# End of the even mixer in a hybrid decoder step: the prompt states of the retention heads go to PSUM bank 0, and norms, roots and roundings are written in another order

## The chip, the cores and the metric

The kernel runs on one core of one Trainium2 chip. The metric is the device time of one execution in microseconds; for the kernel before it is the median of three executions.

## What is computed

One inference step of a two-layer decoder for 512 prompt positions and 8 sample positions that share all weights. Layer 0 has, between two feed-forward blocks, the even mixer: one input projection feeds four retention heads and four HGRN2 heads of 128 x 128, each head's output is normalised and multiplied by a gate, and one output projection takes all eight. Cut to what the change touches:

```python
def even_mixer(h, pos, S_ret0, S_hg0, w_in, w_out, ret_g, hg_g, lb):
    rq, rk, rv, rg, gq, gf, gi, gg = jnp.split(h @ w_in, splits, axis=-1)
    o_r, S_ret = retention_scan(q, k, v, S_ret0, log_gamma)
    o_r = head_norm(o_r, ret_g, False).reshape(B, T, -1) * jax.nn.silu(rg)
    o_g, S_hg = hgrn2_scan(qq, kk, logf, vv, S_hg0)
    o_g = head_norm(o_g, hg_g, False).reshape(B, T, -1) * jax.nn.sigmoid(gg)
    y = jnp.concatenate([o_r, o_g], axis=-1) @ w_out
    return y, S_ret, S_hg
# head_norm: x * lax.rsqrt(jnp.mean(x * x, axis=-1) + EPS) * g
```

## The kernel before

The kernel is one program per engine, written out by hand in order; the engines meet only through semaphores (`wait_ge` ahead of an instruction, `then_inc` on the one that releases). Nothing schedules: the order of the work on an engine is the order of the code. Activations lie transposed, features on partitions and the 520 positions along the free axis. Every large projection multiplies a 128-column unit of the weight, split by ScalarE and VectorE into a rounded part and a rest (`hi`, `lo`), with the likewise split activations, three products for each pair: `three` for most projections, `out_e` for the mixer's output projection.

The change lies between the last unit of the mixer's input projection and the output projection. There a loop over the four retention heads h runs on three engines.

- **TensorE** (from L2143): four score products of head h (L2149, 512, 384, 256 and 128 columns, into banks 1 to 3), the transposes of keys and values of head h+1 (L2100, L2102), the product of weighted scores and values (L2162, bank 6 or 7), the prompt state of head h (L2167, four accumulating 128-column products), and the sum of squares of head h-1 over partitions by a product with ones (L2171). Behind the loop stand 32 one-column products with sample states (L2083), the last sum of squares (L2176), and then the output projection: unit 0 over the four HGRN2 heads, a small sum for the samples (L2089), unit 1 over the HGRN2 heads, then both units over the retention heads, then units 2 to 7 (all L2187).
- **VectorE** (from L1561): `decayed(h)` multiplies the scores by the decay table (L1532, four pieces), `ret_keys(h+1)` scales the transposed keys (L1490), `ret_state(h)` copies the state out of PSUM (L1540). Between them stand `hgrn_norm` for the last HGRN2 head (L1413, L1414), `gated(t)`, which multiplies head t by its gate (L1554; t is 0 to 3 for retention, 4 to 7 for HGRN2), `head_low(t)`, the rest after rounding (L1559), and `ret_norm(h)`: a reciprocal (L1545) and a multiplication (L1546). `sample_out` and `sample_low` do the same for the 8 sample positions.
- **ScalarE** (from L912): it copies the transposed values out (L917), squares the head's output and copies it out of PSUM (L926, L927), takes the root of the sum of squares (`ret_root`, L906), and rounds finished heads (`head_high`, L901).

Buffers tie them together. The state of head h lies in bank 3, in the columns behind the last two score products, and before the next head's scores TensorE waits for its copy:

```python
out = ps[:, min(c + 1, 3), c // 3 * 2 * P:c // 3 * 2 * P + n]
if h and c == 0:
    pe.wait_ge(S("r_p"), NC * h)
    pe.wait_ge(S("st_out"), NH + h)
```

The product of weighted scores and values of heads 2 and 3 writes the PSUM bank that holds head h-2's sum of squares, so it waits for that head's root (`r_sd`). The squares of heads 2 and 3 reuse the buffer that holds the reciprocal root of head h-2, so ScalarE's square waits until that head is normalised and gated (`hn_y`). The weighted scores of head h overwrite those of head h-1, so `decayed(h)` waits for `r_pv`. The two halves of the retention part of the output projection wait for all retention heads and the samples (`hn_lo`, `es_lo`).

## Time and profile before

| | |
|---|---|
| median of 3 executions | 2556.22 us (2552.15 to 2558.25) |
| the profiled execution's own time | 2556.56 us |
| its span | 2554.7 us |
| TensorE busy, share of the span | 2431.4 us, 95% |
| VectorE busy | 1372.7 us, 54% |
| ScalarE busy | 772.8 us, 30% |
| mean granted clock of TensorE | 0.98 |

The span is the time between the first and the last instruction of the profile; 1.9 us of the execution lie around it. Busy TensorE is not TensorE at its peak, since matmuls are pipelined and their ends are modelled. The granted clock is the share of full speed that the engine was given; 0.50 is 1.2 GHz and 1.00 is 2.4 GHz. In the timelines an idle time in square brackets stands ahead of the instruction that ended it, with what released it.

### The profile page before, as it was taken

What the parts mean: (1) busy time and instruction counts of PE and PEld (TensorE: products, weight loads), DVE (VectorE), ACT (ScalarE), POOL (GpSimd) and SP (SyncE); (2) the same over time, 40 slices, a digit from 0 to 9 for tenths busy, and PEclk for the clock granted to TensorE, in tenths of its full rate; (3) what the DMA queues carried; (4) which work ended last, traced back from release to release, by engine and by line L of the source; (5) the groups of instructions that cost most, each with busy time, mean ns of one, the idle gap of its engine ahead of it and who ended that gap; (6) DMA issues with size and microseconds to landing.
All of it is one profiled execution on the core that took longest, in us unless ns stands there. A gap on an engine that the chain in (4) does not pass through costs nothing.

```text
span 2554.7 us, 44447 instructions
## 1 busy us (share of the span) xinstructions
PE 2431.4 (95%) x18881; PEld 2306.1 (90%) x18881; DVE 1372.7 (54%) x1816; ACT 772.8 (30%) x1049; POOL 353.8 (14%) x494
## 2 busy tenths in 40 slices
PE   7999999999889999999999999999988879999999
PEld 6999999999779999999999999887555579999998
DVE  4334334587565444334333437632888855666654
ACT  3222223443323222223222223234333222222222
POOL 1000000232001123000000000001221102444432
PEclk9999999999989999999999999999999899999999
DMA  3333334232114555332333332222444525989974
GB/s 108 91 90 90 104 90 132 76 94 76 45 43 145 160 160 115 96 90 83 90 90 95 101 87 83 83 74 50 129 149 149 157 82 188 297 293 297 300 242 166
DMA packets 444570, 325.19 MB, mean 127 GB/s; under 512 B 14713, under 2 KB 391845, under 8 KB 444301
## 3 DMA queue, kind: packets, MB, share of 16 engines
q1 hardware_dynamic: 427512, 274.90, 36.6%
q0 software_dynamic: 13232, 42.10, 4.6%
q10 hardware_dynamic: 3728, 6.87, 0.8%
q8 instruction: 63, 1.03, 0.2%
q14 instruction: 35, 0.29, 0.0%
HBM read 278.95 MB, written 44.99 MB: 127 GB/s over the span
## 4 chain that ended last, share of the span: by engine, by line
PE 85%; DVE 9%; ACT 2%; issue 2%; DMA 1%; POOL 0%; SPq 0%; DVEq 0%; ACTq 0%; POOLq 0%
PE ps L1921 71%; PE ps L2399 3%; PE ps L2187 2%; PE ps L2373 1%; PE ps L2024 1%; DVE m_qcs L1686 1%; PE ps L2327 1%; DMA m_c_ring<-in_state_mlstm_C 1%; PE ps L2344 1%; DVE m_w_lo L1171 1%; PE ps L2300 0%; PE ps L1985 0%; ACT m_w_hi L700 0%; PE ps L2312 0%; PE ps L2311 0%
## 5 line engine op out<-in xcount | busy, mean ns | idle before, releaser
L1921 PE MATMUL ps<-m_n_hi,m_w_hi 128*128 128x260 f32 x3808 | 772.9, 284 | 13.1 <-DVE m_w_lo L1171 11.5
L1921 PE MATMUL ps<-m_n_hi,m_w_lo 128*128 128x260 f32 x3808 | 768.9, 284 | 0.0
L1921 PE MATMUL ps<-m_n_lo,m_w_hi 128*128 128x260 f32 x3808 | 768.0, 283 | 0.0
L1921 PEld LDWEIGHTS ps<-m_n_hi,m_w_hi 128*128 128x128 f32 x3808 | 589.6, 189 | 16.6 <-DVE m_w_lo L1171 8.9
L1171 DVE TENSOR_TENSOR m_w_lo<-m_w_raw,m_w_hi 128x1024 fp32r<-128x1024 f32 (+1 forms) x312 | 408.3, 1309 | 364.5 <-ACT m_w_hi L700 359.8
L1921 PEld LDWEIGHTS ps<-m_n_hi,m_w_lo 128*128 128x128 f32 x3808 | 588.9, 189 | 0.0
L1921 PEld LDWEIGHTS ps<-m_n_lo,m_w_hi 128*128 128x128 f32 x3808 | 588.0, 189 | 0.0
L700 ACT ACTIVATE m_w_hi<-m_w_raw 128x1024 fp32r<-128x1024 f32 (+1 forms) x312 | 347.6, 1114 | 233.8 <-PE ps L1921 222.7
L1921 PE MATMUL ps<-m_h_hi,m_w_hi 128*128 128x260 f32 x1408 | 283.8, 283 | 0.0
L1921 PE MATMUL ps<-m_h_hi,m_w_lo 128*128 128x260 f32 x1408 | 283.1, 282 | 0.0
L1921 PE MATMUL ps<-m_h_lo,m_w_hi 128*128 128x260 f32 x1408 | 282.5, 282 | 0.0
L1921 PEld LDWEIGHTS ps<-m_h_lo,m_w_hi 128*128 128x128 f32 x1408 | 217.3, 188 | 0.0
L1921 PEld LDWEIGHTS ps<-m_h_hi,m_w_hi 128*128 128x128 f32 x1408 | 216.7, 188 | 0.0
L1921 PEld LDWEIGHTS ps<-m_h_hi,m_w_lo 128*128 128x128 f32 x1408 | 216.6, 188 | 0.0
L733 ACT ACTIVATE m_h_hi<-m_tmp 128x520 f32 (+1 forms) x88 | 56.2, 639 | 370.3 <-DVE m_tmp L1221 370.3
L729 ACT ACTIVATE m_tmp<-m_tmp 128x520 f32<-128x520 f32 x88 | 56.3, 640 | 345.1 <-DVE m_tmp L1206 345.1
L1206 DVE TENSOR_TENSOR m_tmp<-ps,m_rstd 128x520 f32<-128x520 f32 x88 | 61.5, 699 | 161.6 <-PE ps L1921 161.5
L1221 DVE TENSOR_TENSOR m_tmp<-m_tmp,ps 128x520 f32<-128x520 f32 x88 | 61.2, 696 | 148.1 <-PE ps L1921 146.7
L663 POOL TENSOR_SCALAR m_u_ring<-m_u_ring,m_ab 128x512 f32<-128x512 f32 x128 | 100.6, 786 | 230.4 <-DMA m_u_ring<-in_state_mlstm_C 227.7
L709 ACT ACTIVATE m_n_hi<-m_x,m_vec 128x520 fp32r<-128x520 f32 x48 | 35.1, 730 | 276.1 <-DVE m_x L1277 192.2
L1223 DVE TENSOR_TENSOR m_h_lo<-m_tmp,m_h_hi 128x520 fp32r<-128x520 f32 (+1 forms) x88 | 61.9, 704 | 74.8 <-ACT m_h_hi L733 74.8
L1275 DVE TENSOR_TENSOR m_tmp<-ps,m_rstd 128x520 f32<-128x520 f32 x32 | 22.4, 700 | 146.4 <-PE ps L1921 146.4
(432 smaller groups left out, 2573.6 us busy)
## 6 DMA issues: line engine op xcount, KB each, us to landing
m_w_raw<-in_ffn_w_gate SPq DMA_DIRECT2D x88, 512.0 KB, 3.9
m_w_raw<-in_ffn_w_up SPq DMA_DIRECT2D x88, 512.0 KB, 3.8
m_w_raw<-in_ffn_w_down SPq DMA_DIRECT2D x64, 704.0 KB, 4.6
m_c_ring<-in_state_mlstm_C SPq DMA_DIRECT2D x128, 256.0 KB, 3.4
m_u_ring<-in_state_mlstm_C SPq DMA_DIRECT2D x128, 256.0 KB, 6.0
out_C_s<-m_u_ring POOLq DMA_DIRECT2D x128, 256.0 KB, 5.4
m_w_raw<-in_ev_w_in SPq DMA_DIRECT2D x32, 512.0 KB, 4.0
m_w_raw<-in_ml_w_in SPq DMA_DIRECT2D x32, 512.0 KB, 4.0
```

The costliest lines, as they stand in the source:

```text
L663: nc.gpsimd.tensor_scalar(u_ring[:, n % UR, :], u_ring[:, n % UR, :], ab[:, h, 0, b:b + 1], 0.0, ALU.mult, ALU.add)\
L700: nc.scalar.activation(w_hi[:, j % 2, 0:kt * P], w_raw[:, j % 2, 0:kt * P], ACT.Copy).then_inc(S("w_hi"), 1)
L709: nc.scalar.activation(n_hi[:, k, :], x[:, k, :], ACT.Copy, scale=vec1[:, GAIN[s] + k:GAIN[s] + k + 1]).then_inc(S("xn_hi"), 1)
L729: nc.scalar.activation(tmp[c][:, :], tmp[c][:, :], ACT.Silu).then_inc(S("silu"), 1)
L733: nc.scalar.activation(h_hi[:, bass.ds(2 * i + c, 1), :].rearrange("p a t -> p (a t)"), tmp[2 + c][:, :], ACT.Copy).then_inc(S("h_hi"), 1)
L1171: v.tensor_tensor(w_lo[:, j % 2, 0:kt * P], w_raw[:, j % 2, 0:kt * P], w_hi[:, j % 2, 0:kt * P].bitcast(F32), ALU.subtract).then_inc(S("w_ ...
L1206: v.tensor_tensor(two(tmp[c][:, :]), pair(2 * c), by_rstd, ALU.mult).then_inc(S("g_r"), 1)
L1221: v.tensor_tensor(two(tmp[2 + c][:, :]), two(tmp[c][:, :]), pair(2 * c + 1), ALU.mult).then_inc(S("h_f"), 1)
L1223: v.tensor_tensor(h_lo[:, bass.ds(2 * i + c, 1), :].rearrange("p a t -> p (a t)"), tmp[2 + c][:, :], h_hi[:, bass.ds(2 * i + c, 1), :].rea ...
L1921: last = mm(out[:, t, :], w[:, j % 2, c], r[:, k0 + k, t * HT:(t + 1) * HT], start=start and k == 0 and n == 0, stop=stop and k == kt - 1 ...
L2187: last = mm(pair(OUT_E[d])[:, t, :], w[:, d % 2, c], r[:, t * HT:(t + 1) * HT], start=start and k == NH and n == 0, stop=k == NH - 1 and n ...
L2399: last = mm(pair(d % 4)[:, t, :], w[:, i % OS, c], r[:, 4 * q + k, t * HT:(t + 1) * HT], start=q == 0 and k == 0 and n == 0, stop=q == 3 a ...
```

## The change

The prompt states of the retention heads go to bank 0, columns 0 to 127. TensorE's wait for the state copy of head h-1 moves from the scores of head h to the state product of head h; head 0's state product waits for the root of the sample values that lie in bank 0, and the wait for the last copy stands ahead of the one-column products. On VectorE each state copy is moved behind the next head's `decayed` and `ret_keys`, and norms, gates and roundings move behind the loop or one head later. On ScalarE the root of head h-1 is taken ahead of the square of head h for heads 2 and 3, and behind the square for head 1, and the roundings are ordered anew. No instruction is added or taken away, except for waits.

```diff
--- before.py
+++ after.py
@@ -916,6 +916,15 @@
                         act.wait_ge(S("r_st"), h)
                     nc.scalar.activation(r_vtok[(h + 1) % 2], ps[:, 5, :].rearrange("p (c v) -> p c v", c=NC), ACT.Copy)\
                         .then_inc(S("r_vt"), 1)
+                if h == 2:
+                    head_high(NH + 1)
+                if h == 3:
+                    head_high(NH + 2)
+                    head_high(NH + 3)
+                if h >= 2:
+                    ret_root(h - 1)
+                if h == 3:
+                    head_high(0)
                 act.wait_ge(S("r_pv"), h + 1)
                 if h == 0:
                     act.wait_ge(S("g_pv"), NH)
@@ -925,18 +934,16 @@
                     act.wait_ge(S("hn_y"), NH + h - 1)
                 nc.scalar.activation(r_sqb[h % 2][:, :], ps[:, 6 + h % 2, :], ACT.Square)
                 nc.scalar.activation(rv[:, h, 0:TP], ps[:, 6 + h % 2, :], ACT.Copy).then_inc(S("r_o"), 1)
-                if h == 0:
+                if h == 1:
                     sample_high(1)
-                if h:
-                    ret_root(h - 1)
-                head_high(NH + h)
+                    head_high(NH)
+                    ret_root(0)
+            head_high(1)
             ret_root(NH - 1)
-            for t in range(NH):
-                head_high(t)
-                if t == 1:
-                    sample_root(0)
-                if t == 2:
-                    sample_high(0)
+            sample_root(0)
+            head_high(2)
+            sample_high(0)
+            head_high(3)
             for d in range(KD):
                 if 2 <= d + 1 < KD:
                     hi(first_unit["out_e"] + d + 1, (d + 1) % 2, KD)
@@ -1537,7 +1544,7 @@
                 dve.wait_ge(S("r_st"), h + 1)
                 if h == 0:
                     dve.wait_ge(S("st_p_sent"), 16 * NH)
-                v.tensor_copy(st_out[:, h, :], ps[:, 3, 3 * P:TP]).then_inc(S("st_out"), 1)
+                v.tensor_copy(st_out[:, h, :], ps[:, 0, 0:P]).then_inc(S("st_out"), 1)
 
             def ret_norm(h):
 
@@ -1563,28 +1570,30 @@
                 decayed(h)
                 if h + 1 < NH:
                     ret_keys(h + 1)
+                if h:
+                    ret_state(h - 1)
                 if h == 0:
                     lo(first_unit["out_e"] + 1, 1, KD)
                     hgrn_norm(NH - 1)
                     dve.wait_ge(S("g_nm"), NH)
+                if h == 1:
                     gated(NH)
                     sample_out(1)
-                ret_state(h)
-                if h == 1:
+                if h == 2:
                     gated(NH + 1)
                     gated(NH + 2)
                     head_low(NH)
                     sample_low(1)
-                if h == 2:
+                if h == 3:
                     gated(NH + 3)
-                    head_low(NH + 1)
                     ret_norm(0)
                     gated(0)
-                if h == 3:
-                    head_low(NH + 2)
-                    ret_norm(1)
-                    gated(1)
-                    head_low(NH + 3)
+                    head_low(NH + 1)
+            ret_state(NH - 1)
+            ret_norm(1)
+            gated(1)
+            head_low(NH + 2)
+            head_low(NH + 3)
             head_low(0)
             ret_norm(2)
             gated(2)
@@ -2143,7 +2152,6 @@
                     out = ps[:, min(c + 1, 3), c // 3 * 2 * P:c // 3 * 2 * P + n]
                     if h and c == 0:
                         pe.wait_ge(S("r_p"), NC * h)
-                        pe.wait_ge(S("st_out"), NH + h)
                     if h == 0 and c < 2:
                         pe.wait_ge(*evicted(30 + c))
                     mm(out, rk[:, h, c * P:(c + 1) * P], rq[:, h, c * P:TP], start=True, stop=True).then_inc(S("r_s"), 1)
@@ -2163,13 +2171,17 @@
                     at += TP - c * P
                 last.then_inc(S("r_pv"), 1)
                 pe.wait_ge(S("r_kd"), h + 1)
+                if h:
+                    pe.wait_ge(S("st_out"), NH + h)
+                else:
+                    pe.wait_ge(S("es_sd"), 1)
                 for c in range(NC):
-                    last = mm(ps[:, 3, 3 * P:TP], r_etok[h % 2][:, c, :], r_vtok[h % 2][:, c, :], start=c == 0, stop=c == NC - 1)
+                    last = mm(ps[:, 0, 0:P], r_etok[h % 2][:, c, :], r_vtok[h % 2][:, c, :], start=c == 0, stop=c == NC - 1)
                 last.then_inc(S("r_st"), 1)
                 if h:
                     pe.wait_ge(S("r_o"), h)
                     mm(ps[:, 6 + (h - 1) % 2, :], ones[:, :], r_sqb[(h - 1) % 2][:, :], start=True, stop=True).then_inc(S("r_ss"), 1)
-            pe.wait_ge(S("es_sd"), 1)
+            pe.wait_ge(S("st_out"), 2 * NH)
             for m in range(12, 16):
                 state_q(m)
             pe.wait_ge(S("r_o"), NH)
```

The first place is VectorE from the norm of the last HGRN2 head to the scores of retention head 1 (L1413 and L1414 the norm, L1554 its gate, L1467 the samples' reciprocal, L1532 the weighting of the scores). Before:

```order
L1413 RECIPROCAL m_sqb<-m_sqb 128x512 [waits s_g_sd]
L1414 SCALAR_TENSOR_TENSOR m_gi<-m_gi,m_vec_51,m_sqb 128x512 [waits s_dve_own]
L1554 TENSOR_TENSOR m_gi<-m_gi,m_gq 128x512 [waits s_g_nm]
L1467 RECIPROCAL m_qks<-m_qks 128x32 [waits s_es_sd]
L1475 TENSOR_TENSOR m_os<-m_os,m_ggx 128x8
L1540 COPY m_st_out<-ps 128x128 [waits s_st_p_sent,s_r_st]
L1532 TENSOR_TENSOR m_e_p<-ps,m_tab 128x512 [waits s_r_pv,s_r_s]
```

Of the change (L1420 and L1421 the norm, L1539 the weighting, L1497 the keys, L1547 the state copy, L1561 the gate, L1474 the samples):

```order
L1420 RECIPROCAL m_sqb<-m_sqb 128x512 [waits s_g_sd]
L1421 SCALAR_TENSOR_TENSOR m_gi<-m_gi,m_vec_51,m_sqb 128x512 [waits s_dve_own]
L1539 TENSOR_TENSOR m_e_p<-ps,m_tab 128x512 [waits s_r_pv,s_r_s,s_g_nm]
L1539 TENSOR_TENSOR m_e_p<-ps,m_tab 128x384 [waits s_r_s]
L1497 TENSOR_TENSOR m_e_tok<-ps,m_tab 128x512 [waits s_r_st,s_r_tr]
L1547 COPY m_st_out<-ps 128x128 [waits s_st_p_sent,s_r_st]
L1561 TENSOR_TENSOR m_gi<-m_gi,m_gq 128x512
L1474 RECIPROCAL m_qks<-m_qks 128x32 [waits s_es_sd]
```

The weighting of head 1 now stands straight behind the norm, and the state copy, the gate and the samples' operations stand behind it.

The second place is VectorE around the weighting of head 3 (L1532 before). Before, the norm and gate of head 0 (L1545, L1546, L1554) stand ahead of it:

```order
L1540 COPY m_st_out<-ps 128x128 [waits s_r_st]
L1554 TENSOR_TENSOR m_gi<-m_gi,m_ggx 128x512
L1559 TENSOR_TENSOR m_gi_lo<-m_gi,m_gk_hi 128x512 [waits s_hn_hi]
L1545 RECIPROCAL m_e_x<-m_e_x 128x512 [waits s_r_sd]
L1546 SCALAR_TENSOR_TENSOR m_rv<-m_rv,m_vec_51,m_e_x 128x512 [waits s_dve_own]
L1554 TENSOR_TENSOR m_rv<-m_rv,m_gf 128x512 [waits s_r_g,s_dve_own]
L1532 TENSOR_TENSOR m_e_p<-ps,m_tab 128x512 [waits s_r_pv,s_r_s]
L1532 TENSOR_TENSOR m_e_p<-ps,m_tab 128x128 [waits s_r_s]
L1540 COPY m_st_out<-ps 128x128 [waits s_r_st]
L1559 TENSOR_TENSOR m_gi_lo<-m_gi,m_gk_hi 128x512 [waits s_hn_hi]
L1545 RECIPROCAL m_sqb<-m_sqb 128x512 [waits s_r_sd]
```

Of the change, with its line numbers (L1539 weighting, L1547 state copy, L1552 and L1553 norm, L1561 gate, L1566 rounding rest):

```order
L1539 TENSOR_TENSOR m_e_p<-ps,m_tab 128x512 [waits s_r_pv,s_r_s]
L1539 TENSOR_TENSOR m_e_p<-ps,m_tab 128x128 [waits s_r_s]
L1547 COPY m_st_out<-ps 128x128 [waits s_r_st]
L1561 TENSOR_TENSOR m_gi<-m_gi,m_ggx 128x512
L1552 RECIPROCAL m_e_x<-m_e_x 128x512 [waits s_r_sd]
L1553 SCALAR_TENSOR_TENSOR m_rv<-m_rv,m_vec_51,m_e_x 128x512 [waits s_dve_own]
L1561 TENSOR_TENSOR m_rv<-m_rv,m_gf 128x512 [waits s_r_g,s_dve_own]
L1566 TENSOR_TENSOR m_gi_lo<-m_gi,m_gk_hi 128x512 [waits s_hn_hi]
L1547 COPY m_st_out<-ps 128x128 [waits s_r_st]
L1552 RECIPROCAL m_sqb<-m_sqb 128x512 [waits s_r_sd]
```

The norm of head 0 now stands behind the weighting of head 3, and the last state copy stands behind that norm instead of ahead of a rounding rest.

The third place is ScalarE after the square of head 1 (L926 square, L927 copy, L906 root, L901 rounding, L917 values). Before:

```order
L926 ACTIVATE m_sqb<-ps 128x512 [waits s_g_nm,s_r_pv]
L927 ACTIVATE m_rv<-ps 128x512
L906 ACTIVATE m_e_x<-ps,m_lbv 128x512 [waits s_r_ss]
L901 ACTIVATE m_gk_hi<-m_gi 128x512 [waits s_hn_y]
L917 ACTIVATE m_lev_88<-ps 128x512 [waits s_r_st,s_r_tr]
L926 ACTIVATE m_e_x<-ps 128x512 [waits s_hn_y,s_r_pv]
L927 ACTIVATE m_rv<-ps 128x512
L906 ACTIVATE m_sqb<-ps,m_lbv 128x512 [waits s_r_ss]
L901 ACTIVATE m_gk_hi<-m_gi 128x512 [waits s_hn_y]
L926 ACTIVATE m_sqb<-ps 128x512 [waits s_hn_y,s_r_pv]
```

Of the change (L935 square, L936 copy):

```order
L935 ACTIVATE m_sqb<-ps 128x512 [waits s_g_nm,s_r_pv]
L936 ACTIVATE m_rv<-ps 128x512
L896 ACTIVATE m_gk_hi<-m_os 128x4x8 [waits s_es_y]
L901 ACTIVATE m_gk_hi<-m_gi 128x512 [waits s_hn_y]
L906 ACTIVATE m_e_x<-ps,m_lbv 128x512 [waits s_r_ss]
L917 ACTIVATE m_lev_88<-ps 128x512 [waits s_r_st,s_r_tr]
L901 ACTIVATE m_gk_hi<-m_gi 128x512 [waits s_hn_y]
L906 ACTIVATE m_sqb<-ps,m_lbv 128x512 [waits s_r_ss]
L935 ACTIVATE m_e_x<-ps 128x512 [waits s_hn_y,s_r_pv]
L936 ACTIVATE m_rv<-ps 128x512
```

The root of head 1 (into `m_sqb`, L906) stood behind the square of head 2, and now stands ahead of it.

## Rows read from the trace of the kernel before

**Rows 1.** TensorE's timeline: start, us, operation xcount, idle ahead of it

```profile
666.20 2.52 PE L2149 MATMUL ps<-m_rq,m_rk 128*128 128x512 f32 x8
...
671.58 1.06 PE L2167 MATMUL ps<-m_v_tok,m_e_tok 128*128 128x128 f32 x8
677.58 4.61 PE L2149 MATMUL ps<-m_rq,m_rk 128*128 128x512 f32 x8 [4.94 <-DVE m_st_out L1540]
...
693.70 1.02 PE L2171 MATMUL ps<-m_sqb,m_ones 128*128 128x512 f32 x2
...
702.02 4.61 PE L2162 MATMUL ps<-m_e_p,m_lev 128*128 128x512 f32 x8 [5.14 <-ACT m_sqb L906]
...
708.74 4.75 PE L2083 MATMUL ps<-m_qs,m_e_ring 128*128 128x1 f32 x32
714.98 2.08 PE L2176 MATMUL ps<-m_sqb,m_ones 128*128 128x512 f32 x2 [1.49 <-ACT m_rv L927]
...
725.01 0.63 PE L2089 MATMUL ps<-m_qs,m_ones 128*128 128x32 f32 x2 [4.67 <-DVE m_qs L1462]
```

**Rows 2.** Windows: stretch, its length, busy of TensorE, PEld, VectorE, ScalarE, POOL, clock, DMA

```profile
677.00:684.00 7.00, 6.42 (x17) 4.53 (x18) 2.40 (x8) 0.84 (x3) 0.54 (x1) 0.52 0.03 9
...
725.00:731.00 6.00, 5.99 (x26) 5.69 (x26) 5.86 (x7) 0.80 (x2) 0.00 (x0) 0.50 0.00 0
760.00:1000.00 240.00, 240.00 (x1996) 239.78 (x1996) 116.36 (x175) 69.80 (x88) 57.41 (x108) 1.00 0.53 147
```

**Rows 3.** Who VectorE waited for, 666 to 734 us: total, times, longest

```profile
DVE m_st_out L1540 <- PE ps L2167: 11.0, 3, 6.3
...
DVE m_e_p L1532 <- PE ps L2149: 3.9, 5, 2.2
DVE m_rv_lo L1559 <- ACT m_rq_hi L901: 2.4, 2, 1.6
DVE m_gi_lo L1559 <- ACT m_gk_hi L901: 2.3, 1, 2.3
DVE m_e_tok L1490 <- PE ps L2102: 1.1, 1, 1.1
DVE m_lev L1490 <- PE ps L2102: 0.3, 1, 0.3
```

**Rows 4.** ScalarE's timeline: the squares of heads 2 and 3

```profile
700.26 0.60 ACT L926 ACTIVATE m_e_x<-ps 128x512 f32<-128x512 f32 x1 [8.82 <-DVE m_rv L1554]
...
713.84 0.60 ACT L926 ACTIVATE m_sqb<-ps 128x512 f32<-128x512 f32 x1 [11.40 <-DVE m_rv L1554]
```

**Rows 5.** VectorE's timeline: head 0, samples, the weighting of head 3, the last norm

```profile
667.25 0.69 DVE L1532 TENSOR_TENSOR m_e_p<-ps,m_tab 128x512 f32<-128x512 f32 x1 [0.16 <-PE ps L2149]
...
669.62 0.69 DVE L1490 TENSOR_TENSOR m_lev<-ps,m_tab 128x512 f32<-128x512 f32 x1 [0.25 <-PE ps L2102]
...
671.37 3.35 DVE L1413 RECIPROCAL m_sqb<-m_sqb 128x512 f32<-128x512 f32 x1
...
676.14 0.34 DVE L1467 RECIPROCAL m_qks<-m_qks 128x32 f32<-128x32 f32 x1
...
700.09 1.67 DVE L1532 TENSOR_TENSOR m_e_p<-ps,m_tab 128x512 f32<-128x512 f32 x4
...
724.87 3.34 DVE L1545 RECIPROCAL m_sqb<-m_sqb 128x512 f32<-128x512 f32 x1
...
729.04 0.69 DVE L1554 TENSOR_TENSOR m_rv<-m_rv,m_gf 128x512 f32<-128x512 f32 x1
729.65 0.68 DVE L1559 TENSOR_TENSOR m_rv_lo<-m_rv,m_rq_hi 128x512 fp32r<-128x512 f32 x1
```

**Rows 6.** Chain of work that ended last, behind the last rest

```profile
732.93 6.01 PE ps L2187 x48
738.94 1.45 issue
740.39 19.73 PE ps L2187 x163
```

## The prediction

> **What bounds the kernel now.** TensorE is busy for 95% of the span, so I looked first for the stretch where it isn't. From 677 to 725 us its timeline shows it held up four times, by 4.94, 5.14, 1.49 and 4.67 us [rows 1], each time by VectorE or by ScalarE behind it. Besides the idle time, what follows it is slow: the four score products of head 1 take 4.61 us, those of head 0 took 2.52, and the granted clock of the windows behind two of the gaps is 0.52 and 0.50 [rows 2]. From 760 us on TensorE is busy for 240.00 of 240 us.
>
> VectorE's waits in the same stretch [rows 3] add to 21.0 us: 11.0 for state products (it copies a state right after asking for it), 3.9 for scores, 1.4 for transposes, 4.7 for roundings on ScalarE. ScalarE in its turn stands in front of the squares of heads 2 and 3 for 8.82 and 11.40 us, waiting for VectorE's norms of heads 0 and 1 [rows 4]. Head 3 shows the knot: VectorE normalises head 0, ScalarE then squares head 2, copies it and only then takes the root of head 1, 1.76 us from 700.26 to TensorE's start at 702.02 [rows 1, 4], and TensorE's values product of head 3 waits for that root. So the stretch is a ring of three engines that wait for each other. It ends when VectorE's last rest lets TensorE start the retention halves of output units 0 and 1, at 732.93 [rows 6].
>
> **The change, part by part.** VectorE gets the same instructions in another order. So from the last HGRN2 norm at 671.37 [rows 5] its end moves by the idle time that goes, less the idle time that comes. All of it is a schedule by hand.
>
> Head 1: the wait of the scores for the state copy is gone. They run behind head 0's state product, from 672.4 to 674.8, while VectorE is in the norm. The norm takes 4.17 us up to the next operation (724.87 to 729.04, rows 5), so the weighting starts at 675.5 without a wait. TensorE follows at 676.3 with the values product (2.3, half of the 4.61 at the low clock, rows 1), the state and the product with ones (1.06 and 1.02 in their rows, 0.9 each without the overlap of neighbours): scores 2 start at 680.3. VectorE needs 1.67 for the weighting, 0.6 for the keys, 1.44 from the samples' reciprocal over the copy to TensorE's start [rows 1, 5] and 0.6 for the gate: free at 679.8. In head 0 the first weighting stood 1.05 us behind the first score product and the keys 3.42 [rows 1, 5]. So it waits 1.5 us at 679.8 and 0.7 between the pieces: **2.2**.
>
> Head 2: from scores to state product a head took 5.38 us (666.20 to 671.58, rows 1); with 0.9 and 0.9 scores 3 start at 687.5. VectorE has the keys at 683.7, then 0.6, a copy (0.3), two gates and a rest (0.6 each) and the samples' rest (0.1): free at 686.5, next weighting at 688.55. It waits 2.05, and 0.35 between pieces: **2.4**. The root of head 1 now goes ahead of the square of head 2, so the values product of head 3 only follows the weighting, and the 5.14 us gap goes.
>
> Behind that VectorE hardly waits. The state copies come late enough: head 3's state is there at 692.6, its copy stands at 697. Norm and gate of a head take 4.8 us, a rest 0.6 [rows 5]. Norms 1, 2 and 3 start at about 697, 703.4 and 709.4. The roots they need: the square of head 2 still waits for the gate of head 0 (695.9), and TensorE's product with ones can start 1.2 us later (as 713.84 to 714.98, rows 1, 4), at 697.2. That leaves TensorE idle for about 4.5 us, so I take 2.08 as at 714.98: root 2 at about 700. The 32 one-column products, 4.75 us at a mixed clock, end at 704.2, the last product with ones at 706.4, root 3 at 707.1: 2.3 us early. The rounded heads are on time too (head 0 at 700.8, wanted at 702.8). The last retention head waits for the samples' rounding, as before: 0.9.
>
> The sum for VectorE: of idle time 21.0 goes, and 6.1 stands (0.6 of head 0, 2.2, 2.4 and 0.9). That is **14.9 us**. An operation that follows without a wait starts 0.61 us behind the last, where the row's length is 0.69 [rows 5]; with some five fewer breaks that gives 0.4 more: **15.3**. TensorE's start at 732.93 becomes 717.6. Every instruction has been counted and none is new. The four transfers of states to the output, issued by POOL behind the copies, start at about 678, 684, 691 and 697; nothing in the mixer reads them, and they cost nothing.
>
> **What is given back.** By 717.6 TensorE has finished the HGRN2 halves of units 0 and 1: from 706.4, 3.0 us each at full clock (half of 6.01 for 48, rows 6) gives about 712.7, all at the low clock 718. So there is a gap of up to 5 us where before it had waited about 2, and the gaps of 4.94 and 4.67 us both stood ahead of 0.50 windows [rows 1, 2]. No row shows these 48 matmuls at the low clock. Their bounds: 0 if the clock holds. At the low clock throughout unit 0's half costs 3.0 more, and unit 2, which can start 4.4 us behind it (6.01 and 1.45 less 3.0, rows 6), waits for unit 1's 6.0: 1.6 more, together 4.6. Low stretches lasted from 3 to 6 us before, and some of it may fall into the gap itself: I take **1.8**. The Trainium skill (TensorE: Matmul & The Clock Gate, "Why this matters for your kernels") tells to leave no long gaps between bursts of matmuls, since TensorE returns to half rate. The trace agrees at 677 and 725 us. By that rule alone the change, which makes the last gap longer, would pay the whole 4.6 and the gain would be 10.7.
>
> 15.3 less 1.8 is 13.5 us. Behind unit 2 everything is paced by TensorE, busy for 240.00 of 240 us [rows 2], so nothing there can swallow it. The profiled execution, 2556.56 us, becomes 2543.1; it lies 0.3 above the median of 2556.22, which becomes **2542.7**.
>
> **Rivals.**
> - *TensorE becomes the bound of the end* (0.09). If it stays at the low clock from 697 on, it reaches 717.6 with no spare and a late product with ones holds norm 3. For it: the gap ahead of 697.2 and one-column products that hardly load the array. Against: the clock came back behind every gap before. With 4.6 for the clock and 1.5 of lateness the gain is 9.2: 2547.0.
> - *The wait only moves* (0.06). State product h now waits in bank 0 for the copy of state h-1, which VectorE makes behind the next weighting; in TensorE's queue the ones and the next scores stand behind it. By my times the copies of states 0, 1 and 2 are done only 0.5, 1.1 and 0.8 us ahead of the products that wait for them. The skill (PSUM, "Engine vs sequencer instructions") calls VectorE's and ScalarE's queues strictly in order, so nothing overtakes. Where the copies are 3 us late in three heads, 9 of the 15.3 go: with the clock's 1.8 the gain is 4.5, 2551.7.
> - *Slower* (0.03): the clock doesn't come back behind the new last gap, and units 2 to 7 run low. A matmul costs 0.125 us more there (3.0 over 24). From 108 such matmuls on, a bit over two units, the 13.5 are used up; six units of 48 cost 36 us, less 13.5: 2578.7. Against: in every stretch here dense matmuls brought it back within about 6 us.
> - *The change doesn't do what it says*: only if bank 0 is still read when head 0's state is written; the root of the samples there is done before 671, so I give it nothing of its own.
>
> **How the numbers follow.** The forecast has 0.82. Its bounds are gains of 10.7 and 15.3, that is 2540.9 to 2545.5; the three executions spread by 4 us below and 2 above the median, so I open it to 2538.0 and, to take in the first rival, to 2548.5. About 0.2% (5 us) is what a measurement can tell from no change. The forecast, the first rival and a part of the second lie beyond it: faster 0.93, same 0.04, slower 0.03.
>
> **What would show it.** Right: scores of head 1 start near 672.5 without a gap; no wait of TensorE for the root ahead of head 3's values; VectorE's waits between 666 and the end near 6 us, none above 0.3 for state products; the retention half of unit 0 near 717.6 behind a gap of 3 to 5 us, its clock low for a while. Wrong: a state product that waits for a copy, a norm that waits for its root, or a low clock past unit 1.

## The result and the profile after

| | before | after |
|---|---|---|
| median of 4 executions each | 2556.88 us (2552.15 to 2558.25) | 2539.77 us (2538.77 to 2540.84) |
| profiled execution | 2556.56 us | 2540.29 us |
| its span | 2554.7 us | 2538.5 us |

The ratio is 0.9935, interval 0.9923 to 0.9948: 17.1 us faster. A later set of five executions of the same kernel gave 14.0 (below, `e9_change_again`), so the gain is about 14 to 17 us. The forecast was 13.5 (2542.7 us, range 2538.0 to 2548.5); the time fell inside its range, 2.9 us below its centre.

The page of the kernel after, its head: TensorE's work is the same in number of instructions, and 5.0 us less in busy time: head 1's scores and head 3's values, now at the higher clock, are 2.3 us shorter each, and the one-column products 2.1 longer; the rest isn't split up here.

```profile
span 2538.5 us, 44448 instructions
## 1 busy us (share of the span) xinstructions
PE 2426.4 (96%) x18881; PEld 2304.2 (91%) x18881; DVE 1370.4 (54%) x1816; ACT 773.1 (30%) x1049; POOL 362.2 (14%) x494
```

TensorE's timeline after, for [rows 1] (L2157 scores, L2170 values, L2179 state, L2183 and L2188 products with ones, L2092 one-column products, L2199 output projection). The 32 matmuls of L2092 are 16 products of the code (`m` from 12 to 15, four heads each), each recorded as two; the text ahead calls them 32 products:

```profile
672.01 2.32 PE L2157 MATMUL ps<-m_rq,m_rk 128*128 128x512 f32 x8
...
675.90 2.39 PE L2170 MATMUL ps<-m_e_p,m_lev 128*128 128x512 f32 x8 [0.70 <-ACT m_v_tok L917]
678.13 1.06 PE L2179 MATMUL ps<-m_lev,m_lev 128*128 128x128 f32 x8
...
679.88 2.32 PE L2157 MATMUL ps<-m_rq,m_rk 128*128 128x512 f32 x8
...
686.83 2.32 PE L2157 MATMUL ps<-m_rq,m_rk 128*128 128x512 f32 x8
688.98 2.32 PE L2170 MATMUL ps<-m_e_p,m_lev 128*128 128x512 f32 x8
691.14 1.06 PE L2179 MATMUL ps<-m_lev,m_lev 128*128 128x128 f32 x8
696.61 2.07 PE L2183 MATMUL ps<-m_e_x,m_ones 128*128 128x512 f32 x2 [4.41 <-ACT m_rv L936]
698.48 6.83 PE L2092 MATMUL ps<-m_qs,m_e_ring 128*128 128x1 f32 x32
705.16 2.05 PE L2188 MATMUL ps<-m_sqb,m_ones 128*128 128x512 f32 x2
...
716.67 0.50 PE L2199 MATMUL ps<-m_rq_hi,m_w_hi 128*128 128x260 f32 x2 [2.07 <-DVE m_rv_lo L1487]
```

The gaps of 4.94 and 5.14 us ahead of head 1's scores and head 3's values are gone, and so is the low clock behind the first: head 1's scores take 2.32 us where they took 4.61 [rows 1]. One long gap is left, 4.41 us; in it the engine falls to the low clock, where it stays until about 710 us, and from 717.1 to 720.5 us it is there once more. The windows after, for [rows 2] (stretch, its length, busy of TensorE, PEld, VectorE, ScalarE, POOL, clock, DMA):

```profile
676.00:683.00 7.00, 7.00 (x35) 4.93 (x36) 4.87 (x15) 2.40 (x5) 0.54 (x1) 1.00 0.03 9
...
698.50:705.00 6.50, 6.50 (x33) 6.50 (x31) 6.43 (x7) 2.81 (x5) 0.00 (x0) 0.50 0.00 1
705.00:710.00 5.00, 5.00 (x18) 3.97 (x18) 4.86 (x8) 0.69 (x1) 0.00 (x0) 0.50 0.00 0
...
717.30:720.50 3.20, 3.20 (x17) 3.20 (x16) 0.00 (x0) 0.00 (x0) 0.00 (x0) 0.50 0.00 0
720.50:724.50 4.00, 3.69 (x31) 3.47 (x30) 2.22 (x4) 2.21 (x3) 0.00 (x0) 1.00 0.02 4
```

Who VectorE waited for between 666 and 718 us, for [rows 3] (total, times, longest). The 11.0 us for state products and 2.3 for the HGRN2 roundings are gone:

```profile
DVE m_e_p L1539 <- PE ps L2157: 4.1, 4, 2.0
...
DVE m_rv_lo L1566 <- ACT m_rq_hi L901: 0.8, 1, 0.8
...
DVE m_lev L1497 <- PE ps L2111: 0.5, 2, 0.3
```

ScalarE's timeline, for [rows 4]: the squares of heads 2 and 3 (L935) still wait for VectorE's gates, and the root of head 3 (L906) is the operation to watch.

```profile
695.47 0.60 ACT L935 ACTIVATE m_e_x<-ps 128x512 f32<-128x512 f32 x1 [7.76 <-DVE m_rv L1561]
...
701.05 0.60 ACT L935 ACTIVATE m_sqb<-ps 128x512 f32<-128x512 f32 x1 [1.12 <-DVE m_rv L1561]
...
707.25 0.69 ACT L906 ACTIVATE m_sqb<-ps,m_lbv 128x512 f32<-128x512 f32 x1 [4.60 <-PE ps L2188]
```

VectorE's timeline, for [rows 5]: the weightings (L1539) of heads 0, 1, 2 and 3, the norm of head 3 and the wait for the last rounding.

```profile
666.78 0.69 DVE L1539 TENSOR_TENSOR m_e_p<-ps,m_tab 128x512 f32<-128x512 f32 x1 [0.16 <-PE ps L2157]
...
675.06 1.68 DVE L1539 TENSOR_TENSOR m_e_p<-ps,m_tab 128x512 f32<-128x512 f32 x4
...
680.94 1.92 DVE L1539 TENSOR_TENSOR m_e_p<-ps,m_tab 128x512 f32<-128x512 f32 x4 [1.79 <-PE ps L2157]
...
687.88 1.92 DVE L1539 TENSOR_TENSOR m_e_p<-ps,m_tab 128x512 f32<-128x512 f32 x4 [1.98 <-PE ps L2157]
...
708.61 3.34 DVE L1552 RECIPROCAL m_sqb<-m_sqb 128x512 f32<-128x512 f32 x1
...
715.82 0.69 DVE L1566 TENSOR_TENSOR m_rv_lo<-m_rv,m_rq_hi 128x512 fp32r<-128x512 f32 x1 [0.81 <-ACT m_rq_hi L901]
```

And the chain that ended last, for [rows 6]: from the copy of state 2 at 689.8 it now runs on VectorE up to 715.0, then over two roundings on ScalarE, the last rest on VectorE, and 48 matmuls that take 7.52 us instead of 6.01.

```profile
715.27 0.53 ACT m_rq_hi L901
...
716.67 7.52 PE ps L2199 x48
724.19 1.49 issue
725.67 24.40 PE ps L2199 x202
```

**A ruler for the stage.** Whole times spread by some us, so the experiments are read by two lengths in each trace: from VectorE's first weighting to TensorE's start on the retention halves, and from there to unit 2. Before: 667.25 to 732.93 is 65.68, to 740.39 is 73.14. After: 666.78 to 716.67 is 49.89, to 725.67 is 58.89. The first length is shorter by 15.79 us, the second by 14.25. The two spans differ by 16.2: 0.5 of it is the earlier start of the stage, and the last 1.5 lie behind it, where the code is the same (TensorE's waits for `m_acc` in the second mixer are 22.6 us before and 21.5 after). From the start of unit 2 to the end of the span it is 1814.3 us before and 1812.8 after; in the other eleven traces below it is 1812.9 to 1817.2, in no relation to the edits. A gain of two or three us in the stage can be lost in that.

### The profile page after: what moved, and what is told of

Same layout as the page of the kernel before. It is cut to its first block, busy times and chain, and to the rows that moved or that the text cites. A ratio compares the mean times of both kernels' runs of the same rounds, so it can differ in the third digit from the quotient of the medians.

```text
span 2538.5 us, 44448 instructions
## 1 busy us (share of the span) xinstructions
PE 2426.4 (96%) x18881; PEld 2304.2 (91%) x18881; DVE 1370.4 (54%) x1816; ACT 773.1 (30%) x1049; POOL 362.2 (14%) x494
## 4 chain that ended last, share of the span: by engine, by line
PE 87%; DVE 7%; ACT 2%; issue 2%; DMA 1%; POOL 0%; SPq 0%; DVEq 0%; ACTq 0%; POOLq 0%
PE ps L1930 72%; PE ps L2411 3%; PE ps L2199 2%; PE ps L2385 1%; PE ps L2356 1%; PE ps L2339 1%; PE ps L2033 1%; DMA m_c_ring<-in_state_mlstm_C 1%; DVE m_qcs L1695 1%; PE ps L2324 1%; PE ps L2323 1%; DVE m_w_lo L1178 0%; PE ps L2312 0%; PE ps L1994 0%; ACT m_w_hi L700 0%
## 5 line engine op out<-in xcount | busy, mean ns | idle before, releaser
L1930 PE MATMUL ps<-m_n_hi,m_w_hi 128*128 128x260 f32 x3808 | 773.6, 284 | 13.2 <-DVE m_w_lo L1178 11.5
L663 POOL TENSOR_SCALAR m_u_ring<-m_u_ring,m_ab 128x512 f32<-128x512 f32 x128 | 108.9, 851 | 229.3 <-DMA m_u_ring<-in_state_mlstm_C 226.6
```

Source lines behind the costliest of these rows:

```text
L663: nc.gpsimd.tensor_scalar(u_ring[:, n % UR, :], u_ring[:, n % UR, :], ab[:, h, 0, b:b + 1], 0.0, ALU.mult, ALU.add)\
L1930: last = mm(out[:, t, :], w[:, j % 2, c], r[:, k0 + k, t * HT:(t + 1) * HT], start=start and k == 0 and n == 0, stop=stop and k == kt - 1 ...
```

## The experiments

All lengths are in us; "halves" is the first length, "unit 2" the second, the change in brackets is against before.

| run | executions | median | ratio and interval | halves | unit 2 |
|---|---|---|---|---|---|
| `e1_bank` | 10 | 2558.06 | 0.9994 (0.9982 to 1.0006) | 61.15 (-4.5) | 70.14 (-3.0) |
| `e2_root` | 10 | 2555.80 | 0.9988 (0.9978 to 0.9998) | 63.31 (-2.4) | 72.32 (-0.8) |
| `e3_old_act` | 10 | 2552.68 | 0.9979 (0.9969 to 0.9988) | 59.74 (-5.9) | 68.47 (-4.7) |
| `e8_bank_act` | 5 | 2549.30 | 0.9966 (0.9952 to 0.9980) | 56.39 (-9.3) | 66.30 (-6.8) |
| `e4_late_copies` | 4 | 2544.71 | 0.9951 (0.9933 to 0.9969) | 52.20 (-13.5) | 59.66 (-13.5) |
| `e6_double_q` | 5 | 2547.77 | 0.9961 (0.9947 to 0.9975) | 56.08 (-9.6) | 63.54 (-9.6) |
| `e5_filler` | 4 | 2543.91 | 0.9943 (0.9926 to 0.9959) | 49.88 (-15.8) | 58.67 (-14.5) |
| `e9_change_again` | 5 | 2542.94 | 0.9946 (0.9933 to 0.9960) | 49.89 (-15.8) | 57.39 (-15.7) |
| `e7_norm0` | 4 | 2537.52 | 0.9921 (0.9905 to 0.9938) | 46.84 (-18.8) | 55.84 (-17.3) |
| `e10_swap` | 5 | 2539.55 | 0.9934 (0.9920 to 0.9948) | 45.95 (-19.7) | 54.79 (-18.3) |
| `e11_swap_filler` | 5 | 2537.37 | 0.9922 (0.9908 to 0.9935) | 45.94 (-19.7) | 53.40 (-19.7) |

The kernel before had a median of 2559.02 beside `e1` to `e4` (25 executions), 2557.83 beside `e5` to `e8` (9), and 2556.95 beside `e9` to `e11` (9). The three sets ran on three chips. Each ratio is against the kernel before on the same chip; whole times of different sets are not compared closely.

### Which part carries the gain

**The bank alone.** TensorE writes the states to bank 0 and waits as in the change; the orders of VectorE and ScalarE are those of before.

```diff
+                if h:
+                    pe.wait_ge(S("st_out"), NH + h)
+                else:
+                    pe.wait_ge(S("es_sd"), 1)
                 for c in range(NC):
-                    last = mm(ps[:, 3, 3 * P:TP], ...)
+                    last = mm(ps[:, 0, 0:P], ...)
```

> The kernel before with the bank alone: states in bank 0, TensorE's waits as in the change, VectorE's and ScalarE's order untouched. Theory (the order of VectorE is the main part, the bank only makes it possible): the weighting of head 1 starts behind the copy at 677.4 instead of 679.67 and no longer waits between its pieces, the copy of state 1 comes 5.3 us earlier, and the gap of 5.1 us ahead of head 3's values stays. TensorE starts the retention halves 5.3 us earlier than before, the kernel is 5 us faster. Rival (the bank's wait was the cause of the whole stretch): 14 us or more. Rival (the wait only moves to the state product): 0 to 1 us.

Measured: no difference in the whole time, where 5 us were expected (the interval reaches to 4.6 us faster), and in the stage 4.5 of the expected 5.3 us, 3.0 at unit 2. In the profile the 3.0 are lost to a start of the stage 1.2 us later and to 2.9 us more behind unit 2, both in unchanged code. The waits of VectorE from 666 to 736 us say where the rest went:

```profile
DVE m_st_out L1540 <- PE ps L2170: 11.5, 3, 5.5
...
DVE m_e_p L1532 <- PE ps L2148: 0.3, 2, 0.2
```

The waits for scores fall from 3.9 us to 0.3, and VectorE, still copying a state right after asking for it, waits 11.5 for states instead of 11.0 [rows 3]. Head 3's gap on TensorE stays whole:

```profile
699.46 4.33 PE L2161 MATMUL ps<-m_e_p,m_lev 128*128 128x512 f32 x8 [5.15 <-ACT m_sqb L906]
```

**The root alone.** The kernel before, with ScalarE's roots of heads 1 and 2 ahead of the squares of heads 2 and 3.

```diff
+                if h >= 2:
+                    ret_root(h - 1)
                 act.wait_ge(S("r_pv"), h + 1)
...
-                if h:
-                    ret_root(h - 1)
+                if h == 1:
+                    ret_root(0)
                 head_high(NH + h)
```

> The kernel before with ScalarE's root of heads 1 and 2 taken ahead of the next square, nothing else. Theory (VectorE's order holds head 3: its weighting starts only at 700.09, behind the norm of head 0): the values product starts at 700.9 instead of 702.02, about 1.2 us gained. Rival (the root held head 3, as the prediction's paragraph on the ring could be read): the 5.1 us gap goes, 5 us gained.

Measured: 2.4 us of the stage, 1.2 expected. The gap shrinks by 1.1 us only, from 5.14 to 4.04, and has another releaser:

```profile
700.82 3.97 PE L2164 MATMUL ps<-m_e_p,m_lev 128*128 128x512 f32 x8 [4.04 <-DVE m_e_p L1534]
```

The other half comes from less time at the low clock behind the gap: the values product takes 3.97 us instead of 4.61, the state product 1.06 instead of 1.62. So the root was the last arrival at head 3, but close behind stood VectorE's weighting, which before stands behind the norm of head 0. My reading of the knot named only the root; it took both orders to untie it.

**Without ScalarE's order.** The change with ScalarE's program of before (bank and VectorE's order alone).

```diff
-                if h >= 2:
-                    ret_root(h - 1)
...
+                if h:
+                    ret_root(h - 1)
+                head_high(NH + h)
```

> The changed kernel with ScalarE's order of before: bank and VectorE's order alone. Theory: the root of head 1 stands behind the square of head 2, which waits for the gate of head 0, so head 3's values start at 697.2 instead of 688.98, at the low clock; the state copy of head 3, which VectorE makes ahead of norm 1, comes 7 us later, and the rest of head 0 at about 713.5 instead of 702.08. The kernel is 11 us slower than the changed one, 5 to 6 us faster than before. Rival (ScalarE's order is worth the 1.2 us that it is worth alone): 15 us faster than before.

Measured: the stage is 9.85 us longer than with the whole change, about 11 expected. The norm of head 0 now stands behind the weighting of head 3, and ScalarE's root of head 1 still behind the square of head 2, which waits for that norm. TensorE pays in front of head 3's values product (the profile names no releaser; the root it needs, the one behind the square, ends at 698.24 on ScalarE, 0.11 us ahead), and VectorE in front of the copy of state 3:

```profile
698.35 4.09 PE L2163 MATMUL ps<-m_e_p,m_lev 128*128 128x512 f32 x8 [8.09 <-issue]
```

```profile
703.37 0.29 DVE L1540 COPY m_st_out<-ps 128x128 f32<-128x128 f32 x1 [6.28 <-PE ps L2172]
```

**Without VectorE's order.** Bank and ScalarE's order on the kernel before: the edit of `e1_bank`, and ScalarE's lines of the change's diff.

> The kernel before with bank and ScalarE's order of the change, VectorE's order of before. Together with e1 (bank alone, retention halves 4.5 us earlier), e2 (root alone, 2.4) and e3 (bank and VectorE's order, 5.9) it splits the 15.8 us. Theory (the gain needs VectorE's and ScalarE's order together, since head 3's values need the weighting, which VectorE's order makes late, and the root, which ScalarE's makes late): 6 to 8 us earlier than before. Rival (ScalarE's order is the main part): 13 us or more.

Measured: 9.3 us of the stage, more than the 6 to 8 expected. VectorE's order is worth the other 6.5. VectorE still waits for states 10.8 us in three heads, but the 2.3 for the HGRN2 rounding and 1.6 of the retention roundings are gone.

```profile
DVE m_st_out L1547 <- PE ps L2177: 10.8, 3, 4.9
...
DVE m_rv_lo L1566 <- ACT m_rq_hi L901: 0.8, 1, 0.8
```

Together: bank 4.5, root 2.4, bank with VectorE's order 5.9, bank with ScalarE's 9.3, all three 15.8. Once the other two are in, VectorE's order is worth 6.5 and ScalarE's 9.85; alone on the bank they add 1.4 and 4.8. The parts share one ring, and each is worth most when it is the last one put in. VectorE's order cannot run on bank 3: there the scores of head h+1 wait for the copy of state h, and that order makes the copy behind the weighting of those very scores, so both would wait for ever.

### Does the wait only move

**The copies late again.** In the change, the copies of states 0 and 1 stand behind the gates, samples and rests of their heads.

```diff
-                if h:
+                if h == 3:
                     ret_state(h - 1)
...
                     sample_out(1)
+                    ret_state(0)
...
                     sample_low(1)
+                    ret_state(1)
```

> The changed kernel with the copies of states 0 and 1 behind the gates, samples and rests of their step instead of ahead of them. It prices the wait that the change adds. Theory: the copies are only 0.6 and 1.1 us ahead of the state products that wait for them, so the products start 1.35 and a further 0.9 us later, the scores behind them too, and VectorE waits longer for scores: the retention halves start 2.2 us later, the kernel is 2 us slower than the changed one. Rival (there is enough slack in the queues): no difference.

Measured: 2.3 us more in the stage, 2.2 expected. TensorE's state products wait for the copies, and VectorE's next two weightings wait longer for the scores behind them, 3.03 us each instead of 1.79 and 1.98:

```profile
679.54 1.13 PE L2181 MATMUL ps<-m_lev,m_lev 128*128 128x128 f32 x8 [1.01 <-DVE m_st_out L1547]
...
687.54 1.13 PE L2181 MATMUL ps<-m_v_tok,m_e_tok 128*128 128x128 f32 x8 [0.82 <-DVE m_st_out L1547]
```

This is the second rival's mechanism, made on purpose. In the change itself the copies end 0.59, 1.07 and 1.14 us ahead of the products that need them; I had put 0.5, 1.1 and 0.8.

### How near TensorE is to being the bound

**The one-column products twice.**

```diff
             for m in range(12, 16):
+                for h in range(NH):
+                    mm(ps[:, 0, at32:at32 + 1], ..., start=True, stop=True)
                 state_q(m)
```

> The changed kernel with the 32 one-column products issued twice (the same results twice). It measures how near TensorE is to being the bound. The root of head 3 is ready at 707.94 and its norm starts at 708.61, 0.67 us of slack in the profile, not the 2.3 that was predicted. Theory: the doubling costs TensorE 5 to 6.8 us, all but 0.7 reaches the end: 4.5 to 6 us slower than the changed kernel. Rival (VectorE alone is the bound, TensorE has time): under 1 us.

Measured: 6.2 us more in the stage, 4.5 to 6 expected. The 32 added matmuls (16 products of the code) take about 6.8 us, and all but some 0.6 of it reaches the end. TensorE, ScalarE and VectorE:

```profile
714.38 1.84 PE L2092 MATMUL ps<-m_qs,m_e_ring 128*128 128x1 f32 x8
716.08 2.05 PE L2192 MATMUL ps<-m_sqb,m_ones 128*128 128x512 f32 x2
```

```profile
718.17 0.69 ACT L906 ACTIVATE m_sqb<-ps,m_lbv 128x512 f32<-128x512 f32 x1 [11.44 <-PE ps L2192]
```

```profile
718.89 3.35 DVE L1552 RECIPROCAL m_sqb<-m_sqb 128x512 f32<-128x512 f32 x1 [1.92 <-ACT m_sqb L906]
```

In the change the root of head 3 ends at 707.94 and the norm that needs it starts at 708.61: 0.67 us to spare. I had put 2.3. This is the ring's next stop, and the first rival was nearer than the prediction's margin of 2.3 us made it look.

### The clock behind the last gap

**Fillers in the gap.** Sixteen products into an unused bank behind unit 1's HGRN2 half, ahead of the wait for the samples.

```diff
             out_e(1, range(NH, KD), True)
+            pe.wait_ge(S("r_sd"), NH)
+            for i in range(16):
+                mm(ps[:, 7, 0:HT], w_hi[:, 1, 0:P], e_hi(NH)[:, 0:HT], start=True, stop=True)
             pe.wait_ge(S("es_lo"), 2)
```

> The changed kernel with 16 extra products of 260 columns into the free bank 7 on TensorE, between the HGRN2 half of unit 1 and the wait for the last rest; they compute nothing that is used. Theory (the low clock in the retention halves comes from the 2.07 us gap and the weak load ahead of it): the 48 matmuls take 6.0 us instead of 7.52, unit 2 starts 1.2 us earlier against the weighting of head 0, and the kernel is 1 us faster. Rival (the low clock has another cause, or the extra products run over the start): no difference or slower by their 2 us.

Measured: nothing to tell from the change; the 1 us expected did not come. The fillers ran for 2.06 us, a gap of 1.76 stayed, and some 1.4 us into the halves the clock fell all the same:

```profile
714.50 2.06 PE L2211 MATMUL ps<-m_gk_hi,m_w_hi 128*128 128x260 f32 x16
718.32 0.51 PE L2199 MATMUL ps<-m_rq_hi,m_w_hi 128*128 128x260 f32 x2 [1.76 <-DVE m_rv_lo L1487]
```

**The change unchanged**, as a control for the set that follows.

> The changed kernel unchanged, on the same chip as the two runs beside it, to compare them with and to see how much of the 17.1 us was the spread of the first timing. The spans of the profiles differ by 16.2 us. Theory: 14 to 17 us faster than before.

Measured: the length to the halves is 49.89 us, the same to the hundredth, behind a gap of 2.87 us; but the 48 matmuls take 6.05 us where the first profile had 7.52:

```profile
721.26 6.05 PE ps L2199 x48
727.31 1.45 issue
```

So the 1.5 us of the clock are not a fixed price of the change: one kernel shows both, and in this one the longer gap has the faster matmuls. Over all the traces the gap ahead of the halves and the 48 matmuls are: held at 6.0 behind 0.56 (`e11`), 1.58 (`e4`), 1.93 (before), 2.25 (`e6`) and 2.87 (`e9`); 7.5 to 7.6 behind 1.76 (`e5`), 1.93 (`e3`), 2.06 (`e1`), 2.07 (after), 2.20 (`e2`), 3.65 (`e10`) and 4.56 (`e7`); 8.57 behind 4.06 (`e8`). The falls cost 1.5 to 1.6 us, even behind the gap of 4.56, and 2.6 in `e8`. Between 1.6 and 2.9 us both are seen, and the gap's length doesn't sort them. What decides there stays open.

### A better order

**Norm of head 0 between two weightings.** In the change VectorE waits 1.79 and 1.98 us for scores. Here the three HGRN2 gates stand ahead of weighting 2, and the norm and gate of head 0 between weightings 2 and 3; the rests stand behind weighting 3.

```diff
                 if h == 1:
                     gated(NH)
                     sample_out(1)
-                if h == 2:
                     gated(NH + 1)
                     gated(NH + 2)
+                    gated(NH + 3)
+                if h == 2:
+                    ret_norm(0)
+                    gated(0)
+                if h == 3:
                     head_low(NH)
                     sample_low(1)
-                if h == 3:
-                    gated(NH + 3)
-                    ret_norm(0)
-                    gated(0)
                     head_low(NH + 1)
```

> The changed kernel with VectorE's three gates of HGRN2 heads 1 to 3 ahead of the weighting of head 2 (1.8 us, where it waits 1.79 for scores), and norm and gate of head 0 (4.8 us) between the weightings of heads 2 and 3 in place of two gates and two rests (2.5 us, and 1.98 of wait); the rests move behind. Theory (VectorE's sum of work and waits sets the stage): 3.6 us of its waits go, the retention halves start 3.5 us earlier, the low clock behind a longer TensorE gap gives up to 1 us back: 2.5 to 3.5 us faster than the changed kernel. Rival (TensorE, which has 0.67 us of slack, becomes the bound): under 1 us. That is unlikely since its 4.41 us gap ahead of the product with ones goes too.

Measured: 3.05 us less than the change, both to the halves (3.5 expected) and to unit 2. In whole time its interval overlaps that of the change. Both waits for scores and the 4.41 us gap of TensorE are gone; new are 0.38 us of TensorE ahead of head 3's values, 2.01 ahead of the last product with ones, and 0.98 of VectorE ahead of the last copy:

```profile
689.78 1.67 DVE L1539 TENSOR_TENSOR m_e_p<-ps,m_tab 128x512 f32<-128x512 f32 x4
...
693.93 0.29 DVE L1547 COPY m_st_out<-ps 128x128 f32<-128x128 f32 x1 [0.98 <-PE ps L2179]
```

**And the last rounding first.** `e7_norm0` with ScalarE's rounding of head 3 ahead of that of the samples.

```diff
             head_high(2)
-            sample_high(0)
             head_high(3)
+            sample_high(0)
```

> e7 (norm of head 0 between the weightings of heads 2 and 3) and, on ScalarE, the rounding of retention head 3 ahead of the samples' rounding instead of behind it. The last rest of head 3 waited 0.81 us for that rounding in every kernel so far. Theory: that wait goes, the samples' rest hides behind the last rest, the retention halves start 0.7 to 0.8 us earlier than in e7, 3.8 us earlier than in the changed kernel; the kernel is 3 to 4 us faster than the changed one. Rival (the samples' rounding then comes late): no difference to e7.

Measured: 0.9 us less to the halves than `e7_norm0`; the wait of 0.81 is gone. The whole time can't tell the two apart: the intervals overlap, and they ran on different chips. Beside the change on its own chip it is 3.4 us faster (2539.55 against 2542.94), 3 to 4 expected, with intervals that overlap too.

**And fillers.** `e10_swap` with 26 fillers at the place of `e5_filler`.

> e10 with 26 unused products of 260 columns on TensorE in the gap of about 3 us ahead of the retention halves, so that hardly any gap is left. In e5 16 of them left 1.76 us of a gap, and the clock fell all the same 1.5 us into the halves (7.56 us for 48 matmuls). Theory (a gap of any size at an unlucky moment lowers the clock; none doesn't): 6.0 us for the 48, unit 2 starts 1.2 to 1.4 us earlier than in e10. Rival (the clock falls from something else than the gap): 7.5 us again, no difference or slightly slower.

Measured: the same length to the halves, and 1.4 us less to unit 2. The fillers leave a gap of 0.56 and the 48 matmuls take 6.01:

```profile
709.05 3.25 PE L2211 MATMUL ps<-m_gk_hi,m_w_hi 128*128 128x260 f32 x26
712.85 0.50 PE L2199 MATMUL ps<-m_rq_hi,m_w_hi 128*128 128x260 f32 x2 [0.56 <-DVE m_rv_lo L1487]
```

It is the shortest stage of all, 19.7 us below before at unit 2, and in whole time 19.6 below before and 5.6 below the change beside it (2537.37 against 2542.94, all five executions of the one below all five of the other). That the fillers hold the clock rests on one trace; their 2.2 us in the medians are within what such sets spread by.

## Why the prediction was right, step by step

- **The ring of three engines**: right. Each engine's order alone gives a part of it (1.4 to 4.8 us on top of the bank), all together 15.8.
- **Head 1** (scores behind head 0's state product, from 672.4; weighting without a wait at 675.5; scores 2 at 680.3): measured 672.01, 675.06 and 679.88. The stage began 0.47 us earlier, so these are right within 0.1 us. The last arrival at head 1's values product was ScalarE's copy of the transposed values, by about 0.1 us, which the prediction doesn't name.
- **Waits of 2.2 and 2.4**: 1.79 and 1.98 in front; the weightings take 1.92 instead of 1.68, so 0.24 between the pieces of each; and 0.25 ahead of the keys of head 2. That is 2.28 and 2.22. Head 0 has 0.56 (0.6 forecast), the last rounding 0.81 (0.9).
- **The sum for VectorE**: idle time of 5.9 us stands where I had 6.1, which makes 15.1. The measured 15.8 leaves 0.7 for the overlap of neighbours, where I took 0.4.
- **Head 3's knot, "only then takes the root of head 1"**: right as far as it went, and incomplete. `e2_root` shows the weighting behind the norm of head 0 as the next obstacle, 1.1 us behind. The forecast was not hurt, because the change moved both and the sum counted both.
- **"The 32 one-column products, 4.75 us at a mixed clock"**: this term was mis-sized. They ran wholly at 0.50 and took 6.83 us; at 1.00 they take 3.63 (`e7_norm0`). So the root of head 3 was 0.67 early and not 2.3. It cost nothing because the slack took it, and `e6_double_q` shows that nearly nothing of it was left.
- **"A gap of up to 5 us" ahead of 717.6**: it was 2.07. TensorE finished the HGRN2 halves at 714.6, since it had come 0.8 us late to them (707.2 instead of 706.4) and ran the first 3.8 us of them low, as the window from 705 to 710 us shows. Start of the retention halves: 717.6 forecast, 716.67 measured, of which 0.47 is the earlier start of the stage.
- **The clock's 1.8, with bounds of 0 and 4.6**: 1.5 in the first profile (7.52 less 6.01), and 0 in the second of the same kernel. That the estimate came near was luck: its reason, a gap of up to 5 us, did not occur, since the gap was about as long as before. Its other reason, "low stretches lasted from 3 to 6 us before", is read too low: windows of 1 us show each of the kernel's four low stretches there lasting nearly 7 us, part of it in the gap (for example from 700.9 to 707.7). The Trainium skill (TensorE: Matmul & The Clock Gate, "Why this matters for your kernels") says to leave no long gaps between bursts of matmuls, as they bring the half rate back, and by that rule alone the forecast's gap would have cost the whole 4.6. No trace of the change shows more than 1.5, and behind the 4.56 us gap of `e7_norm0` it was 1.5 too.
- **State transfers cost nothing; nothing behind unit 2 swallows the gain**: right. In the trace only POOL waits for the four copies, and nothing in the mixer waits for their transfers. Of the 2.8 us between the forecast for the profiled execution (2543.1) and its 2540.29, 0.75 lie in the stage, 0.5 in its start, and 1.5 behind it in unchanged code. The control set's median, 2542.94, is 0.2 from the forecast; the two sets say how far such a number can be trusted.
- **The rivals**: TensorE as the bound and the moved wait did not occur, but both were near (0.67 us and 0.6 us of slack). Slower did not occur: the clock was back at 720.5 us, 4 us into the halves.

## What to carry to other kernels

Where engines wait for each other in a ring, sum the idle time of the engine whose work has to be done in any case, and lay out its new order with the rows' durations: here that gave the stage to half a us, though the bank alone was worth 4.5 of the 15.8 us and the root alone 2.4. Before believing a slack, size TensorE's work at the lower clock too: here 6.83 us stood where 4.75 had been taken, behind a gap of 4.41. And an operation that nobody waits for soon (here the long norm) belongs in the place where the engine would wait, not behind the waits: that gave another 3 us of the stage.

## What the hardware did that I had not expected

**The clock fell while TensorE was busy.** Windows of the kernel before, over its one-column products:

```profile
708.70:711.00 2.30, 2.30 (x22) 2.26 (x21) 2.30 (x2) 0.00 (x0) 0.51 (x1) 1.00 0.08 29
711.00:713.50 2.50, 2.49 (x13) 2.40 (x12) 2.43 (x3) 0.00 (x0) 0.00 (x0) 0.50 0.00 0
```

There was no gap between the two, and the granted clock went from 1.00 to 0.50; the last gap ahead of them, 5.14 us, had ended at 702.02, and the clock had been back since about 707.7. In the kernel after, TensorE was recorded busy for 6.50 of 6.50 us on the same kind of products and stayed at 0.50 throughout; in `e6_double_q` 64 of them ran at one pace, 8 in 1.84 us. In the kernel after, 260-column matmuls stood in front of both returns to 1.00, near 710 and 720.5 us. But one-column products do not go with the low clock everywhere: in `e7_norm0` the same 32 ran wholly at 1.00:

```profile
694.59 3.63 PE L2092 MATMUL ps<-m_qs,m_e_ring 128*128 128x1 f32 x32
```

So no run here shows what made the clock fall at 711 us.

**The same gap, two clocks.** Behind gaps of 1.93 us the 48 matmuls took 6.01 in the kernel before and 7.56 in `e3_old_act`; in the change they took 7.52 behind 2.07 and 6.05 behind 2.87. A single profile is not enough to price a gap of this size.
